# Output tiles scaled and turned token-major one by one, with the norm applied last per partition

## The reference

```python
merged = jax.nn.sigmoid(g_a) * br_a + jax.nn.sigmoid(g_b) * br_b
x = x + gate[:, None, :] * (merged @ w_o[l])
return rms_norm_2(x, final_g)

def rms_norm_2(x, g):
    xf = x.astype(jnp.float32)
    y = xf * lax.rsqrt(jnp.mean(xf * xf, axis=-1, keepdims=True) + NORM_EPS)
    return (y * g.astype(jnp.float32)).astype(x.dtype)
```

## Time and profile before

| | us |
|---|---|
| median of 3 runs | 1757.54 (1755.89 to 1759.77) |
| the profiled execution | 1760.88 |
| its span, first to last instruction | 1759.1 |
| PE busy in it | 1597.7 (91%) |
| DVE busy in it | 824.5 (47%) |
| ACT busy in it | 780.4 (44%) |
| POOL busy in it | 777.5 (44%) |
| mean granted clock of TensorE | 0.956 |

### The profile page before, as it was taken

The page is one execution under the profiler, slowest core; times in us unless marked ns, Lnnn a source line. Parts: engine busy times, 40 slices in busy tenths (PEclk is TensorE's granted clock), DMA queues, the critical chain, the costliest instruction groups (busy, mean ns, idle before and its releaser), DMA issues. The chain is left out here.

```text
span 1759.1 us, 30287 instructions
## 1 busy us (share of the span) xinstructions
PE 1597.7 (91%) x12030; PEld 1290.4 (73%) x12030; DVE 824.5 (47%) x1664; ACT 780.4 (44%) x1424; POOL 777.5 (44%) x469
## 2 busy tenths in 40 slices
PE   4899999999999998699999986999977898699996
PEld 2688888888888886477777775666767786588875
DVE  3224342434434254445655533259636753475534
ACT  3535445363544534255456543245664442332221
POOL 2635345262433523264555442234747650365551
PEclk7999999999999999899999998999998998799998
DMA  4524232232323221244444212323100000333331
GB/s 97 148 61 115 69 99 72 75 109 62 108 65 100 72 62 32 66 144 135 138 124 131 84 36 63 107 69 70 37 14 3 4 4 3 104 100 96 93 87 48
DMA packets 245988, 136.60 MB, mean 78 GB/s; under 512 B 24286, under 2 KB 239342, under 8 KB 245783
## 3 DMA queue, kind: packets, MB, share of 16 engines
q1 hardware_dynamic: 217080, 107.11, 22.1%
q10 hardware_dynamic: 28768, 27.54, 5.4%
HBM read 132.11 MB, written 2.52 MB: 77 GB/s over the span
## 5 line engine op out<-in xcount | busy, mean ns | idle before, releaser
L819 POOL TENSOR_TENSOR a_w_low<-a_w_raw,a_w_high 128x1024 fp32r<-128x1024 f32 x88 | 211.4, 2415 | 91.8 <-ACT a_w_high L656 91.8
L292 PE MATMUL a_proj<-h_low,a_w_high 128*128 128x512 f32 x512 | 208.3, 407 | 16.9 <-DVE h_low L866 12.6
L294 PE MATMUL a_proj<-h_high,a_w_high 128*128 128x512 f32 x512 | 202.5, 396 | 0.0
L293 PE MATMUL a_proj<-h_high,a_w_low 128*128 128x512 f32 x512 | 201.6, 394 | 0.0
L839 POOL TENSOR_TENSOR a_sq_low<-a_sq,a_sq_high 128x512 fp32r<-128x512 f32 x48 | 62.1, 1293 | 276.0 <-ACT a_sq_high L691 275.9
L819 POOL TENSOR_TENSOR b_w_low<-b_w_raw,b_w_high 128x1024 fp32r<-128x1024 f32 x40 | 99.8, 2497 | 118.1 <-ACT b_w_high L656 118.1
L2526 POOL TENSOR_TENSOR f_w_low<-f_wt,f_w_high 128x1024 fp32r<-128x1024 f32 x40 | 96.0, 2401 | 122.8 <-ACT f_w_high L2482 122.8
L292 PE MATMUL b_proj<-h_low,b_w_high 128*128 128x512 f32 x320 | 132.8, 415 | 15.1 <-DVE h_low L866 13.8
L292 PEld LDWEIGHTS a_proj<-h_low,a_w_high 128*128 128x128 f32 x512 | 96.9, 189 | 45.1 <-POOL a_w_low L819 11.9
L294 PE MATMUL b_proj<-h_high,b_w_high 128*128 128x512 f32 x320 | 128.5, 402 | 0.0
L293 PE MATMUL b_proj<-h_high,b_w_low 128*128 128x512 f32 x320 | 127.7, 399 | 0.0
(11 more groups left out here) (384 smaller groups left out, 3994.0 us busy)
## 6 DMA issues: line engine op xcount, KB each, us to landing
a_w_raw<-in_a_w_in_dram SPq DMA_DIRECT2D x80, 512.0 KB, 3.8
b_w_raw<-in_b_w_in_dram SPq DMA_DIRECT2D x32, 512.0 KB, 4.2
b_ada_w<-in_ada_w_dram ACTq DMA_DIRECT2D x24, 512.0 KB, 3.6
f_wt<-in_w_in_dram SPq DMA_DIRECT2D x24, 512.0 KB, 3.8
a_bias<-scr_a ACTq DMA_DIRECT2D x16, 576.0 KB, 4.7
sparse_w_raw<-in_w_in_dram SPq DMA_DIRECT2D x17, 512.0 KB, 3.8
a_w_raw<-in_a_w_out_dram SPq DMA_DIRECT2D x8, 512.0 KB, 3.9
b_w_raw<-in_b_w_out_dram SPq DMA_DIRECT2D x8, 512.0 KB, 3.8
```

Source lines behind the costliest of these rows:

```text
L292: nc.tensor.matmul(out, lh, rl, start=first, stop=False)
L293: nc.tensor.matmul(out, ll, rh, start=False, stop=False)
L294: return nc.tensor.matmul(out, lh, rh, start=False, stop=last)
L819: nc.gpsimd.tensor_tensor(wl[:, slot_of(b), :, :], raw[:, n % RAW, :, :], wh[:, slot_of(b), :, :], ALU.subtract).then_inc(s_wl, 1)
```

## The change

Three pieces move. Each updated tile of X is multiplied at once by its column of `fg` (128x512, into one of two buffers `scaled`), PE turns that tile with four transposes into one PSUM bank `turned`, after the following out product, and DVE copies the bank into `otok`, at a stride, so that all four token blocks get their 128 features. ACT's squares are made between the tiles instead of behind them. The sums of squares are taken by eight matmuls of 128x128 by one column of ones, four on the running sum of squares 0 to 6 and four on the last square, so that the result is 128x4, one number per partition (token) for each of four token blocks. Ln and Exp run on 128x4. Last, DVE multiplies token blocks 0 and 2 of `otok` by their column of `rn`, ACT blocks 1 and 3, 128x1024 each, and SP stores each block when it is done. SP's order of issues is unchanged: `fg` still comes behind the 40 blocks. The core of the diff:

```diff
-        sq, rn = sb("sq", [P, 2, SEQ]), sb("rn", [P, SEQ])
+        sq, rn = sb("sq", [P, 2, SEQ]), sb("rn", [P, 4])
+        scaled = sb("scaled", [P, 2, SEQ])
...
-        ps_ss = pb("ss", [P, 512])
+        ps_ss, ps_t = pb("ss", [P, 512]), pb("turned", [P, 512])
...
             for r in range(4):
-                sp.wait_ge(s_tok, 2 * r + 2)
+                sp.wait_ge(s_norm[r % 2], r // 2 + 1)
                 sp.dma_start(out[0, r * P:(r + 1) * P, :], otok[:, r, :]).then_inc(s_out, 16)
...
+            def turn(k):
+                pe.wait_ge(s_o, k + 1)
+                if k:
+                    pe.wait_ge(s_tok, k)
+                for r in range(4):
+                    mm = nc.tensor.transpose(ps_t[:, r * P:(r + 1) * P], scaled[:, k % 2, r * P:(r + 1) * P], T.ident)
+                mm.then_inc(s_turn, 1)
+
+            def sum_tokens(x, k, first):
+                if first:
+                    pe.wait_ge(s_acc, k)
+                else:
+                    pe.wait_ge(s_sq, k + 1)
+                for r in range(4):
+                    mm = nc.tensor.matmul(ps_ss[:, r:r + 1], x[:, r * P:(r + 1) * P], T.ones[:, 0:1], start=(first and r == 0),
+                                          stop=(r == 3 and not first))
+                if not first:
+                    mm.then_inc(s_ss, 1)
...
-            pe.wait_ge(s_acc, KT - 1)
-            nc.tensor.matmul(ps_ss[:, :], T.ones, T.rn[:, :], start=True, stop=True).then_inc(s_ss, 1)
-            pe.wait_ge(s_o, KT)
-            for n in range(8):
-                r, half = n // 2, n % 2
-                if n >= BANKS:
-                    pe.wait_ge(s_tok, n - BANKS + 1)
-                for q in range(4):
-                    mm = nc.tensor.transpose(ps[n % BANKS][:, q * P:(q + 1) * P], X[:, 4 * half + q, r * P:(r + 1) * P], T.ident)
-                mm.then_inc(s_turn, 1)
+                if kind == "out" and j:
+                    turn(j - 1)
+            turn(KT - 1)
+            sum_tokens(T.rn[:, :], KT - 2, True)
+            sum_tokens(sq[:, (KT - 1) % 2, :], KT - 1, False)
...
+                if kind == "out" and j:
+                    square(j - 1)
+            square(KT - 1)
             act.wait_ge(s_ss, 1)
-            nc.scalar.activation(rn[:, :], ps_ss[:, :], ACT.Ln, scale=1.0 / D, bias=T.eps[:, 0:1]).then_inc(s_ln, 1)
+            nc.scalar.activation(rn[:, :], ps_ss[:, 0:4], ACT.Ln, scale=1.0 / D, bias=T.eps[:, 0:1]).then_inc(s_ln, 1)
             act.wait_ge(s_ln, 1)
             nc.scalar.activation(rn[:, :], rn[:, :], ACT.Exp, scale=-0.5).then_inc(s_r, 1)
+            act.wait_ge(s_r, 1)
+            act.wait_ge(s_tok, KT)
+            for r in (1, 3):
+                nc.scalar.activation(otok[:, r, :], otok[:, r, :], ACT.Copy, scale=col(rn, r)).then_inc(s_norm[1], 1)
...
+            def keep_token_major(k):
+                dve.wait_ge(s_turn, k + 1)
+                nc.vector.tensor_copy(otok[:, :, k * P:(k + 1) * P],
+                                      ps_t[:, :].rearrange("p (r n) -> p r n", r=4)).then_inc(s_tok, 1)
...
+                    dve.wait_ge(s_take, n + 1)
+                    if j == 0:
+                        dve.wait_ge(s_small, 16)
+                        dve.wait_ge(s_y, KT)
+                    if j >= 2:
+                        dve.wait_ge(s_turn, j - 1)
+                    nc.vector.tensor_scalar(scaled[:, j % 2, :], X[:, j, :], col(fg, j), None, ALU.mult).then_inc(s_o, 1)
                     if j >= 2:
                         add_square(nc, dve, T, sq, s_sq, s_acc, j - 1)
-            add_square(nc, dve, T, sq, s_sq, s_acc, KT - 1)
-            dve.wait_ge(s_take, len(plan))
+                    if j:
+                        keep_token_major(j - 1)
+            keep_token_major(KT - 1)
             dve.wait_ge(s_r, 1)
-            dve.wait_ge(s_small, 16)
-            for k in range(KT):
-                nc.vector.scalar_tensor_tensor(out=X[:, k, :], in0=X[:, k, :], scalar=col(fg, k), in1=rn[:, :],
-                                               op0=ALU.mult, op1=ALU.mult).then_inc(s_o, 1)
-            for n in range(8):
-                dve.wait_ge(s_turn, n + 1)
-                nc.vector.tensor_copy(otok[:, n // 2, n % 2 * 512:(n % 2 + 1) * 512], ps[n % BANKS][:, :]).then_inc(s_tok, 1)
+            dve.wait_ge(s_tok, KT)
+            for r in (0, 2):
+                nc.vector.tensor_scalar(otok[:, r, :], otok[:, r, :], col(rn, r), None, ALU.mult).then_inc(s_norm[0], 1)
```

More of the change, by code:

```diff
@@ L2405, in merge @@
         s_acc = sem("squares_added")
+        s_norm = [sem("normal_dve"), sem("normal_act")]
         s_sq, s_ss, s_ln, s_r, s_o, s_turn, s_tok = (
@@ L2482, in split_high, with square @@
                 nc.scalar.activation(wh[:, b % SPLIT, :, :], ring.at(b), ACT.Copy).then_inc(s_wh, 1)
+            def square(k):
+                act.wait_ge(s_take, len(plan) - KT + k + 1)
+                if k >= 3:
+                    act.wait_ge(s_acc, k - 2)
+                nc.scalar.activation(sq[:, k % 2, :] if k else T.rn[:, :], X[:, k, :], ACT.Square).then_inc(s_sq, 1)
             for b in range(SPLIT):
```

## The result

| | before | after |
|---|---|---|
| median | 1758.41 us (6 runs, 1755.89 to 1759.77) | 1765.58 us (6 runs, 1765.18 to 1766.83) |
| profiled execution | 1760.88 | 1765.18 |
| its span | 1759.1 | 1763.4 |

The ratio is 1.0045, with a 95% interval of 1.0034 to 1.0056: slower by 0.45%, 7.2 us. The forecast was 1764.5, +0.40%, within 1760.0 to 1769.0.

What follows compares the result with a forecast made beforehand. TensorE (PE), busy 91%, was taken to bound the kernel until the last product, then a 20.3 us tail. 8.6 + 1.7 + 2.9 - 6.2 = +7.0 us on the median 1757.54 gave 1764.5 us (+0.40%), range 1760.0 to 1769.0.

Steps and rivals of the forecast that it cites:

- The stall: Ahead of the first transposes, behind product 1: PE stands still until the late gains land and DVE scales; 8.6 us lost.
- The clock: Behind PE's idle time at product 1: matmuls run at the 1.2 GHz level for a stretch; 1.7 us lost, bounds 0 to 3.4.
- The turnings: Between out products 1 and 7: six groups of four transposes on PE at 0.48 us each; 2.9 us more.
- The cover on DVE: Tiles 2 to 4: DVE's copy ends near +5.0, before PE wants it at +5.7; hidden, with 0.7 us to spare.
- The tail: From X's last update to the end: first store 6.6 us earlier, stores closer together; 6.2 us gained.
- the share for a low clock: In the tail: a third of the 2.3 us that transposes and sums would lose at low clock; 0.8 us charged.
- The sum: Whole kernel: 8.6 + 1.7 + 2.9 - 6.2 = +7.0 us.
- The rival "faster": At the first transposes: the gains land in time, so stall and clock loss fall away; 1754.2 us, chance 5%.
- One bound in that rival: Ahead of the first transposes: the change turns faster from a stall below 3.3 us, given as a landing before 1709.2.

Runs made afterwards that it cites:

- e1: The changed kernel with the load of the final gains issued behind weight block 2 instead of block 39; 1753.86 us, ratio 0.9984 to the kernel before.
- e2: The kernel before, with DVE also waiting for the final gains behind its update of output tile 0; 1758.28 us, ratio 1.0002 to the kernel before.
- e5: The changed kernel, gains still loaded late, with all eight groups of transposes on PE behind the last product; 1752.52 us, ratio 0.9967 to the kernel before.
- e3: The changed kernel with 80 transposes of the identity, read by nobody, on PE behind out product 1; 1764.23 us, ratio 1.0040 to the kernel before.
- e4: The kernel of e1 with every group of four transposes into the turned bank issued twice; 1757.56 us, ratio 1.0001 to the kernel before.
- e7: The kernel of e1 with three more 128x512 additions on DVE in each of tiles 2, 3 and 4; 1756.75 us, ratio 0.9992 to the kernel before.

## Why the prediction was right

**The stall (forecast 8.6 us).** Transfer, chain and place were as said. `fg` was issued 3.91 us behind the mark, landed 3.8 us later, and the scaling took 486 ns where 0.48 was interpolated. Between the last matmul slot of product 1 and the first transpose are 8.57 us (the same place before lies 0.26 ahead of the mark: 1703.31; 1711.88 - 1703.31). e1 shows that the load's place is the cause, e2 that DVE's wait alone is not, e5 that PE's queue is what hands it on.

**The clock (forecast 1.7, bounds 0 to 3.4).** From the first transpose to product 2's end it took 8.31 us where the later products, at full clock, are 5.91 apart: 2.4. The step was mis-sized by 0.7: the one row it was taken from the earlier trace rows was a slow stretch that ended after 3.75 us, and this one went on for some 5. e3 measured it apart: 2.34.

**The turnings (forecast 0.48 each, 2.9 in all).** The later products are 5.91 us apart instead of 5.44: 0.47 each, times six 2.8. The forecast's split of that price was off: it took 0.095 a transpose and 0.1 for the change of kind, and e4 shows 0.109 a transpose and next to nothing for the change (0.44 for four more).

**The cover on DVE (forecast 0.7 us to spare).** In tile 2 of the changed kernel the addition of a square took 2.47 us beside POOL's 2.40, and the copy ended 4.74 us behind X's update, where +5.0 was forecast and PE came for it at +5.7. These are the rows:

```profile
1721.59 2.40 POOL L2550 TENSOR_TENSOR f_w_low<-f_wt,f_w_high 128x1024 fp32r<-128x1024 f32 x1 [14.54 <-ACT f_w_high L2498]
1722.06 2.47 DVE L286 TENSOR_TENSOR rn<-rn,f_sq 128x512 f32<-128x512 f32 x1 [0.40 <-ACT f_sq L2504]
1724.45 0.68 DVE L2584 COPY Y<-f_turned 128x512 f32<-128x512 f32 x1
```

By these rows 1.0 us was to spare. e7 shows the edge: 1.85 us more on DVE made PE start turning 2 0.98 us late. By the Trainium skill (SBUF — State Buffer, Who interferes with whom) the second of VectorE and GpSimd to ask for their shared port pair waits until the first is done. The traces agree for both kinds of instruction: the addition with two SBUF inputs took 2.47 us in the changed kernel, where it started behind POOL's subtraction, and the scaling in e7, once it came second, 2.54 us.

**The tail (forecast 6.2 less, 7.0 before the share for a low clock).** 20.32 became 13.46: 6.9 less. First store at 6.51 behind X's last update (6.3 forecast), from there 6.95 to the end (6.9 forecast). The share of 0.8 for the clock was too careful: only the last of the sums ran slower (1.25 us for eight records, 1.03 in e1_gains_early, whose tail is 0.20 shorter). The windows of the stores show 410 GB/s. The Trainium skill (DMA: Bandwidth & Descriptors, Specifications) gives about 358 GB/s as one core's limit to HBM; here, with one core at work, the stores went beyond it.

```profile
1758.00:1759.00 1.00, 0.00 (x0) 0.00 (x0) 0.00 (x0) 0.00 (x0) 0.00 (x0) 0.50 1.01 410
...
1760.00:1761.00 1.00, 0.00 (x0) 0.00 (x0) 0.00 (x0) 0.00 (x0) 0.00 (x0) 0.50 1.02 410
```

**The sum.** 8.57 + 2.4 + 2.8 - 6.9 = 6.9 us against 7.0 forecast. Two misses cancelled: 0.7 more for the clock, 0.7 more gained in the tail, so that the sum is closer than two of its terms, by luck. The rival "faster" needed the gains in time; e1 is that case, and against 1754.2 forecast for it stands 1753.86. Its traces put it at 4.2 us below the kernel before where 3.3 was forecast, for the tail gave more. One bound in that rival was misread: a stall below 3.3 us needs a landing before 1708.7, not 1709.2, since the scaling and the hand-overs (0.55 us) come between. It changes no chance, as even the issue came later than either.

## What to carry to other kernels

When work is moved ahead, look up when each of its inputs arrives, the small ones too: here 4 KB at the end of SP's queue, whose issue hung on the very product behind which PE then waited. A wait on an engine with time to spare is free until an engine without any has an instruction queued behind its outcome; look at that hand-over, not at the wait. And "as soon as it is ready" is no gain by itself: the transposes cost PE the same between the products as behind them, and behind the last product part of them ran beside work that had to be done anyway.

## What the runs showed of the hardware that was not expected

The same pause of 2.17 us, before the last matmuls of out product 0, met with different clocks. In the kernel before it was followed by a granted clock of 0.52, as in eight of the others by the length of products 0 and 1 together (10.1 to 10.2 us from ACT's last merged high half to the mark), but in e4_double_turns the clock stayed up and this stretch took 8.6. That alone moves an execution by 1.6 us. The timeline of e4_double_turns at that pause, and its windows behind it:

```profile
1693.71 0.50 PE L292 MATMUL f_p<-f_merged_low,f_w_high 128*128 128x512 f32 x1 [2.17 <-POOL f_merged_low L2556]
```

```profile
1693.00:1695.00 2.00, 1.29 (x6) 1.07 (x7) 0.28 (x1) 0.23 (x1) 0.66 (x1) 1.00 0.15 44
1695.00:1697.00 2.00, 2.00 (x10) 1.67 (x9) 0.96 (x2) 0.83 (x1) 1.09 (x1) 1.00 0.00 0
```

What decides between the two was not tried. The load of 4 KB took 3.7 to 4.0 us to land in the five kernels in which it stands behind one weight block, and 5.9 behind three that were issued just ahead of it in e1_gains_early, where nobody waited for it.
